# Routing tail of a decoder trunk on one core: experts chosen inside cross-attention's last rounds, one-hots made by eights, a reordered beginning, and identity products issued in waits

## The reference, cut to what matters

```python
for l in range(DEPTH):                                   # DEPTH = 1, SEQ = 2048, D_MODEL = 1024, float32
    h = rmsnorm(x, norm_mix[l]); z = h @ w_in[l]         # u_a, v_a, q_b, k_b, v_b: 512 columns each
    y_a = chunk_gmlp(u_a, v_a, v_norm[l], w_spatial[l], b_spatial[l])
    y_b = stick_breaking_attention(q_b, k_b, v_b)
    x = x + concat(rmsnorm(y_a), rmsnorm(y_b)) @ w_out[l]
    h = rmsnorm(x, norm_cross[l]); m = rmsnorm(mem, norm_mem[l])
    x = x + memory_cross_attention(h, m, w_xq[l], w_xk[l], w_xv[l], w_xo[l])
    h = rmsnorm(x, norm_moe[l])
    x = x + hierarchical_moe(h, w_group[l], b_group[l], w_router[l], b_router[l], w1[l], w3[l], w2[l])
return rmsnorm(x, norm_final)

def hierarchical_moe(h, ...):                            # 4 groups of 8 experts, 2048 tokens
    g_logits = t @ w_group + b_group                     # top-1 group
    e_logits = t @ w_router + b_router                   # top-2 experts inside that group
    gates = softmax(g_logits)[chosen] * softmax(top_2 of e_logits)
    # tokens sorted by expert, each expert padded to blocks of 128 tokens,
    # each block: (silu(xb @ w1[e]) * (xb @ w3[e])) @ w2[e], added back with its gate
```

## Time and profile before

| | us |
|---|---|
| median of 3 runs (2696.63 to 2699.92) | 2697.1 |
| the profiled execution: its own time | 2697.8 |
| its span, first to last instruction | 2696.1 |
| TensorE busy in the span | 2529.0 (94%) |
| VectorE busy | 1478.6 (55%) |
| ScalarE busy | 1275.4 (47%) |
| GpSimd busy | 626.4 (23%) |
| mean granted TensorE clock | 0.971 of full |

### The profile page before, as it was taken

The page is one execution under the profiler, slowest core; times in us unless marked ns, Lnnn a source line. Parts: engine busy times, 40 slices in busy tenths (PEclk is TensorE's granted clock), DMA queues, the critical chain, the costliest instruction groups (busy, mean ns, idle before and its releaser), DMA issues. The chain is left out here.

```text
span 2696.1 us, 44306 instructions
## 1 busy us (share of the span) xinstructions
PE 2529.0 (94%) x14282; PEld 2030.8 (75%) x14283; DVE 1478.6 (55%) x1959; ACT 1275.4 (47%) x2254; POOL 626.4 (23%) x682
## 2 busy tenths in 40 slices
PE   7999999899999999999999999579999999999991
PEld 6888888676666778786888888468887888888881
DVE  5221344698888954444333332566988754555643
ACT  4221211698898931143222222135878654465543
POOL 0000011477777710000000000222222212112123
PEclk9999999899999999999999999689999999999996
DMA  6433240313101033233112121428999855586757
GB/s 237 165 137 125 83 157 32 98 45 142 64 17 45 2 137 117 87 150 110 64 71 86 70 86 51 192 97 292 383 382 369 297 200 197 192 289 201 260 159 268
DMA packets 141436, 414.79 MB, mean 154 GB/s; under 512 B 22016, under 2 KB 30720, under 8 KB 140288
## 3 DMA queue, kind: packets, MB, share of 16 engines
q1 hardware_dynamic: 124896, 370.63, 36.9%
q0 software_dynamic: 13968, 33.59, 5.3%
q10 hardware_dynamic: 2448, 8.91, 0.8%
HBM read 338.60 MB, written 91.75 MB: 160 GB/s over the span
## 5 line engine op out<-in xcount | busy, mean ns | idle before, releaser
L656 POOL TENSOR_TENSOR stick_weight<-stick_weight,stick_left 128x512 f32<-128x512 f32 (+3 forms) x320 | 328.3, 1040 | 126.5 <-DVE stick_left L786 122.1
L1716 DVE TENSOR_TENSOR moe_w_lo<-moe_w_lo_raw,moe_w_hi (+1 forms) x256 | 297.9, 1219 | 59.1 <-ACT moe_w_hi L1712 31.3
L1712 ACT CAST moe_w_hi<-moe_w_lo_raw (+1 forms) x256 | 255.0, 1051 | 45.9 <-DMA moe_w_lo_raw<-in_w 27.7
L786 DVE TENSOR_TENSOR_SCAN stick_left<-stick_z_ps,stick_left,stick_any_row 128x512 f32<-128x512 f32 x192 | 240.1, 1274 | 35.4 <-ACT stick_z_ps L749 35.1
L747 ACT ACTIVATE stick_weight<-stick_z_ps 128x512 f32<-128x512 f32 (+3 forms) x320 | 173.7, 543 | 32.7 <-PE stick_z_ps L696 21.1
L709 PE MATMUL stick_t_ps<-all_ident,stick_weight 128*128 128x128 f32 x1088 | 165.4, 281 | 18.6 <-ACT stick_weight_t L756 9.2
L749 ACT ACTIVATE stick_z_ps<-stick_z_ps 128x512 f32<-128x512 f32 (+3 forms) x320 | 165.7, 518 | 10.2
L709 PEld LDWEIGHTS stick_t_ps<-all_ident,stick_weight 128*128 128x128 f32 x1088 | 116.0, 141 | 69.4 <-issue 45.8
L64 PE MATMUL exp_g_ps<-moe_w_hi,exp_x_hi 128*128 x376 | 153.9, 409 | 11.4 <-DVE exp_x_lo L2153 11.4
L1727 POOL DMA_INDIRECT moe_xg<-hm_scratch,moe_now x50 | 61.5, 1229 | 408.6 <-PE exp_x_ps L2189 275.4
L64 PE MATMUL exp_y_ps<-moe_w_hi,exp_h_hi 128*128 128x512 f32 x376 | 152.1, 405 | 2.3 <-DVE exp_h_lo L2173 2.3
(11 more groups left out here) (280 smaller groups left out, 5807.0 us busy)
## 6 DMA issues: line engine op xcount, KB each, us to landing
moe_w_lo_raw<-in_w SPq DMA_DIRECT2D x384, 512.0 KB, 12.4
proj_w_lo_raw<-in_w_in SPq DMA_DIRECT2D x40, 256.0 KB, 6.3
proj_xs<-in_x SPq DMA_DIRECT2D x16, 512.0 KB, 4.7
qt_scratch<-proj_qk_out SPq DMA_DIRECT2D x16, 512.0 KB, 3.1
kt_scratch<-proj_qk_out SPq DMA_DIRECT2D x16, 512.0 KB, 2.7
mix_q<-qt_scratch SPq DMA_DIRECT2D x16, 512.0 KB
mix_out_xs<-in_x SPq DMA_DIRECT2D x16, 512.0 KB, 4.4
x_scratch<-mix_out_xs SPq DMA_DIRECT2D x16, 512.0 KB, 3.0
```

Of the source, the lines that this page charges most:

```text
L656: nc.gpsimd.tensor_tensor(taken, taken, after, ALU.mult).then_inc(weight_done, 1)
L786: nc.vector.tensor_tensor_scan(row[:, c * BANK:c * BANK + keys][:, ::-1], back, any_row[:, 0:keys], start, ALU.mult, ALU.bypass).then_inc( ...
L1712: nc.scalar.copy(self.w13_hi[:, self.w13_at(e, i)], self.w13_raw[:, self.w13_at(e, i)]).then_inc(self.w13_cut, 1)
L1716: ops.tensor_tensor(self.w13_lo[:, self.w13_at(e, i)], self.w13_raw[:, self.w13_at(e, i)], as_f32(self.w13_hi[:, self.w13_at(e, i)]), ALU. ...
```

## The change

Six edits. The first is new text for TensorE: `keep_busy` issues `count` products of the identity with itself into a PSUM area that nobody reads, in seven places: 22 at the start of `project`, 14 at its end, 16 in round -1 of cross, 16 at the start of `route`, 20 ahead of the one-hot products, and 20 ahead of and 20 behind the first transpose of `run_experts`.

The second reorders the beginning of `project`: the gains' load moves from ScalarE's to SyncE's list, behind x tile 0; turn 1 moves on TensorE into the middle of `(V, 0, 0)`; x tile 3 is loaded ahead of the K weights, for which SyncE waits for turn 0; tile 4 is squared and normed one turn later, behind the cutting of Q.

Third, SyncE's wait for the stores of `ya` moves from the end of `project` to the second head pair of `attend_stick`, and `y_out` gets memory of its own.

Fourth, the choice becomes `Picks.choose(first, count)` with 21 instructions and `pick` in bfloat16. Round 15 of cross chooses for tiles 0 to 13, round 16 for tile 14, and `route` only for tile 15.

Fifth, one-hots are made eight token tiles at a time by VectorE alone, 4 chunks of 4 instructions, two chunks ahead; GpSimd's part goes. Sixth, in `route` ScalarE takes the exponential of `ratio` ahead of all eight cuts of expert 0 instead of between four and four.

```diff
+def keep_busy(pe, out, ident, count):
+    for _ in range(count):
+        pe.matmul(out, ident, ident, start=True, stop=True)
...
                 load_x(0)
+                sp.dma_start(gains[:], gain.partition_broadcast(P)).then_inc(gains_loaded, 16)
                 load_w(V)
                 load_x(1)
                 load_x(2)
                 load_w(Q)
+                sp.wait_ge(ht_done, 1)
+                load_x(X_SLOTS)
                 load_w(K)
...
-                for i in range(2):
-                    sp.wait_ge(y_stored[i], 16 * tiles // 2)
...
-                act.dma_start(gains[:], gain.partition_broadcast(P)).then_inc(gains_loaded, 16)
...
+                        if n == 0 and r == rows // 2 - 1:
+                            turn(1)
...
                 pe.wait_ge(masked, 3)
+                keep_busy(nc.tensor, mix_ps[:, 0], ident, 22)
...
                 mix(tiles - 1)
+                keep_busy(nc.tensor, ht_ps[:, 0], ident, 14)
...
                     if pair == 1:
+                        for i in range(2):
+                            sp.wait_ge(loads.y_stored[i], 16 * tiles // 2)
                         out_loads.load_first(nc, sp)
...
+                    if is_last(b):
+                        dve.wait_ge(logit_out, tiles - 2)
+                        picks.choose(nc, link, 0, tiles - 2)
+                    if isinstance(b, int) and b == tiles:
+                        dve.wait_ge(logit_out, tiles - 1)
+                        picks.choose(nc, link, tiles - 2, 1)
                     if there(b, -1):
                         dve.wait_ge(logit_done, b)
...
                     if there(b, 1):
+                        if isinstance(b, int) and b == -1:
+                            pe.wait_ge(vo_ready, rows)
+                            keep_busy(nc.tensor, x_ps[:, 0:P], ident, 16)
                         pe.wait_ge(p_done, b + 2)
...
+                for c, (k, first) in enumerate(chunks):
+                    span = slice(first, first + CHUNK)
+                    rows_wide, slots_wide = [P, CHUNK, blocks], [P, CHUNK, P]
+                    if c >= DEPTH:
+                        dve.wait_ge(slotted, (c - DEPTH + 1) * CHUNK)
+                    of_token, of_gate = in_block[:, c % DEPTH, :, 0], in_block[:, c % DEPTH, :, 1]
+                    nc.vector.tensor_tensor(of_gate, block_no[:].unsqueeze(1).broadcast_to(rows_wide),
+                                            dest_part[:, 0, k, span].unsqueeze(2).broadcast_to(rows_wide), ALU.is_equal).then_inc(marked, 1)
+                    nc.vector.tensor_tensor(in_slot[:, c % DEPTH], lanes[:].unsqueeze(1).broadcast_to(slots_wide),
+                                            dest_part[:, 1, k, span].unsqueeze(2).broadcast_to(slots_wide), ALU.is_equal).then_inc(marked, 1)
+                    dve.wait_ge(marked, 2 * c + 1)
+                    nc.vector.tensor_tensor(of_token, of_gate, token[:, span].unsqueeze(2).broadcast_to(rows_wide), ALU.mult).then_inc(weighed, 1)
+                    dve.wait_ge(weighed, 2 * c + 1)
+                    nc.vector.tensor_tensor(of_gate, of_gate, gates[:, k, span].unsqueeze(2).broadcast_to(rows_wide), ALU.mult).then_inc(weighed, 1)
...
+                keep_busy(nc.tensor, g_ps[:, 0:P], ident, 20)
                 transpose_x(0)
+                keep_busy(nc.tensor, g_ps[:, 0:P], ident, 20)
```

More of the change, by code:

```diff
@@ L563, in __init__ @@
         self.q_loaded = [s.sem(f"q_loaded{g}") for g in range(self.chunks)]
+        self.y_stored = [s.sem(f"y_stored{i}") for i in range(2)]
     def other_chunks(self, s):
@@ L1270, in attend_memory @@
         s = Scope(nc, stack, "cross")
+        h_hi, h_lo = s.sbuf("h_hi", [P, rows, P], F32R), s.sbuf("h_lo", [P, rows, P], F32R)
+        p_parts = s.sbuf("p_parts", [P, 2, rows, P], F32R)
+        at = s.next_at()
+        wq_t = s.sbuf("wq_t", [P, 2, rows, P])
+        picks = Picks(s, at, logits, n_group, consts, tiles - 2)
+        assert picks.end <= at + 8 * rows * P
         sk_hi, sk_lo = s.sbuf("sk_hi", [P, rows, width], F32R), s.sbuf("sk_lo", [P, rows, width], F32R)
@@ L1314, in rounds, with is_last @@
                 step(b, b % 2)
+        def is_last(b):
+            return isinstance(b, int) and b == tiles - 1
         def is_first(b):
@@ L1591, in turn_hm @@
                     transposes(s_ps, hm_sb, tm_done)
-                def is_last(b):
-                    return isinstance(b, int) and b == tiles - 1
                 def step(b, slot):
@@ L1828, in _ @@
-                for g in range(n_group):
-                    span = slice(g * members, (g + 1) * members)
-                    wide_g = [P, tiles, members]
-                    link(nc.vector.tensor_tensor(e_in[:, :, span], logits[:, :, n_group + g * members:n_group + (g + 1) * members],
-                                                 g_pick[:, :, g:g + 1].broadcast_to(wide_g), ALU.mult))
-                    link(nc.vector.tensor_tensor(e_in[:, :, span], e_in[:, :, span], shut[:, :, g:g + 1].broadcast_to(wide_g), ALU.add))
@@ L1843, in _ @@
-                link(nc.vector.tensor_tensor(both[:], pick[:, 0], pick[:, 1], ALU.add), "both")
+                picks.choose(nc, link, tiles - 1, 1)
                 link(nc.vector.tensor_tensor(ratio[:], e_top[:, 1], e_top[:, 0], ALU.subtract), "ratio")
```

176 lines of the change are left out of this document (98 added, 78 removed).

## The result

The changed kernel takes 2665.97 us (median of 4 runs, 2664.14 to 2666.16) against 2696.92 us: a ratio of 0.9881, 95% interval 0.9864 to 0.9898. The profiled execution has a span of 2664.4 us, and its own time is 2666.2 us.

The account below looks back on a forecast made before the run. TensorE, busy 94% of the span, was taken as the bound, with only its gaps and low clock to gain from. Terms -4.8 - 1.7 - 1.6 - 9.1 - 3.3 + 0.3 = -20.2 from 2697.8 gave 2677.6 us, range 2672 to 2684.5.

Parts of the forecast that it names:

- Beginning: Start of `project`: the gap ahead of turn 1 goes, `(V, 0, 0)` ends near 21.5; -4.8 us (3.0 to 6.3).
- Stores' wait: End of `project`: SyncE's wait for the last `ya` store, which holds everybody, goes; -1.7 us (1.5 to 2.0).
- First round of cross: Cross's first round: 16 identity products fit the 4.5 us gap and keep the clock up; -1.6 us (0 to 1.7).
- End of cross: Last rounds of cross, up to `route`: no change in the low clock costed, 0 us.
- Choices: `route`: choices for tiles 0 to 14 hidden in cross, one-hots start 15.1 us in, not 24.2; -9.1 us (7.9 to 10.0).
- One-hots: One-hot stretch: four chunks of 3.5 us plus last products, 16.9 us instead of 20.2; -3.3 us (2.3 to 4.2).
- Experts' start: First expert product: identity products delay it 2.0 us, the full clock returns 1.7; +0.3 us (-1.7 to +2.6).
- Behind it: From block 1's first product to the end of the span: no gain forecast, 0 us.
- rival 4: End of cross and behind block 0: clock holds there too, two times 1.7 us, 2674; chance 0.07 with "more".
- rivals, 1: All identity-product places: they get in the way as the clock stays low; 2699.3 in full (0.02), 2681 to 2686 partly (0.06).
- Rival 2: Round 15 of cross: something waits for VectorE's 14-tile choice; up to 10.9 us, 2688.5; chance 0.04.
- Rival 3: Experts' stage, 2010 to 2110: weights arrive barely in time, a shifted phase adds a few us; 2681; chance 0.07.

Follow-up runs that it names:

- order_only: Kernel before, with only cross's h_hi, h_lo, p_parts and wq_t allocated ahead of sk and vo; 2690.5 us, ratio 0.9972.
- low_apart: Changed kernel with two pads putting cross's h and p_parts 64 bytes apart from sk and vo modulo 256; 2674.2 us.
- no_cross_identity: Changed kernel without the 16 identity products in cross's first round, the other six places kept; 2666.7 us.
- experts_same: Changed kernel with a 960-byte pad putting the experts' x and h at their weights' offset; 2652.6 us, ratio 0.983 to the kernel before.
- high_same: Kernel before with two pads: cross's h high at sk's offset, p_parts high, 128 past vo modulo 256; 2691.2 us, one run.

## Why the prediction was wrong

The step that failed stands in its first paragraph: "The change takes no product out of it, so only what lies in its gaps, or runs at its lower clock, can be gained." There was a third thing. The split products of cross, 96 in each of 16 rounds, became 2.4% shorter from start to start, 7.9 us in the trace; order_only showed it alone (-7.5 us) and low_apart took it away (+8.2). The move of the four tensors is in the full diff, and was costed at nothing without a word. With it the sum would have been -28.1, at 2669.7, and the range would have reached down to 2664.1, below the 2666.0 measured.

It could have been seen before: in the timeline of the kernel before the products of `project` start 0.226 us apart at the full clock (23.97 to 26.91 is thirteen of them), and twelve in cross take 2.8 us, 0.233 each. A kind of instruction with two rates in one trace was a question to ask.

The terms, in their order:

- **Beginning** -5.05 for -4.8, which the prediction had put between 5.6 (the clock holds) and 3 (it falls for the second half). It fell in the first half, from 15.3 to 18.7, where VectorE's norm of tile 1 set the pace, and was full for the second. The steps of the 5.6 each took a little more: turn 1 started at 18.21 for 17.8, and with the second half it took 3.9 us for 3.7. The norm of tile 0 was done by 8.7, sooner than the 9.6 of the text, and turn 0 started behind the identity products at 10.27 for 9.9. How much of the term they make is open: in five other traces with them the clock rose sooner and turn 0 started at 8.7 to 9.5.
- **Stores' wait** -2.1 for -1.7, within its bounds but for 0.1. SyncE waits for no store at the end of `project`.
- **First round of cross** -1.9 for -1.6: the clock is 1.00 where it was 0.53. **End of cross** +1.1 for 0: the low clock behind the 2.5 us wait at 1668 lasted twice as long, 6.8 us for 3.4, where the forecast had costed no change; no_cross_identity shows that such stretches come and go from trace to trace.
- **Choices** -8.7 for -9.1: right in its steps. For tiles 0 to 13 the 21 instructions ended 10.7 us after they began (10.9 forecast), with 5.5 us to spare ahead of the next work; the ranks began 6.4 us in (6.1), the one-hots 15.5 (15.1).
- **One-hots** -5.4 for -3.3, the term that was mis-sized. A chunk took 3.12 us, not 3.5: the durations were 0.1 us shorter in sum (1.22 for 1.23, 0.70 for 0.74), and three of the four instructions start some 0.1 us before the row of the one ahead ends, which a sum of durations counts twice, 0.2 us a chunk. Four chunks, 1.5 us. The rest is the clock, which was full at the end (0.91 on average over the stretch), so that the last products took 2.0 us, near the 1.8 of the full clock, where the sum had taken the middle of 1.8 and 3.7. That VectorE gets no quicker per element held. The Trainium skill, "VectorE: DVE Perf Modes", section "The perf-mode tier table", has a `tensor_scalar` in float32 at twice the rate of a `tensor_tensor`. By half of its 2293 ns for 2048 elements, an estimate, the `tensor_tensor` of 1024 takes 1.15 us; the trace has 1.22, against 0.75 for one tensor operand, which agrees in direction but is 1.6 times and not twice.
- **Experts' start** +0.3 for +0.3, and as forecast: first product 12.6 us after the low parts began (12.7), 1.8 us after its operands were ready, and the full clock gave it back.
- **Behind it** -1.6 for 0: the low clock behind block 0, part of the 0.89 in the earlier trace rows, did not come, which was rival 4 in part. In experts_same and no_cross_identity it did, with the same identity products, so this was luck.

Of the rivals, 1 did not come in full: no group of identity products ran at the lower clock to its end (22 products took 8.0 us for 7.5, the two groups of 20 at the experts' start 7.5 and 4.6), and the kernel without them is no faster. Rival 2 did not: the choices had 5.5 us to spare. Rival 3 did not in this change, but it did in experts_same, where the slow blocks around 2000 take back 5.8 of 18.4 us.

## What to carry to other kernels

Where TensorE is bound by products of 512 columns in float32r, put the stationary and the moving operand at the same offset modulo 256 bytes. It costs a pad, and gave 7.5 us in one stage and 13.4 us in another here, less where the loads of weights set the pace; look first for one kind of product that starts at two rates in one trace. In reading a diff, an allocation that moves is a change as well: it wants a line in the sum. And identity products that hold the clock have to be measured with many executions: seven places gave 1.5 to 2.6 us together, which is within the noise here.

## What the runs showed of the hardware

- The time from one float32r product of 128x128 by 512 to the next, at the full clock, depends on the distance of its two SBUF operands modulo 256 bytes: 227 ns at 0, 229 at 192, 232 at 128, 233 at 32 and 64. It depends neither on the absolute offset (704 and 768 both gave 227) nor on whether the stationary operand lies low (the changed kernel) or high (high_same) in SBUF. Why is open: nothing here looks inside, and no other distance was tried.
- At the lower clock the distance costs nothing: in the kernel before the products of cross (64 apart) and of `project` (0 apart) both start every 426.7 ns there.
- The stretches at the low clock behind a wait of 2.5 or 4.6 us differ between kernels that have the same work in front of them: 0, 3.4 or 6.8 us in the traces here. That they differ between executions of one kernel too is likely but not shown, as each has one trace. Four executions of one kernel were 6 us apart (2663.8 to 2670.1), where those of the changed kernel were 2 us apart.
- Back to back on VectorE, an instruction that does not wait starts some 0.1 us ahead of the end of the one before it (1715.66 against 1715.03 + 0.71); the sum of durations of a chunk's four was 0.2 us too long.
